# Experts' up products in halves of 32 tokens and four column groups, the second half under a branch

## What is computed

```
def _moe(h, w_router, b_router, w1, w3, w2):
    ...
    best = jnp.argmax(grp_score, axis=-1)
    in_group = (jnp.arange(N_EXPERTS) // EXPERTS_PER_GROUP)[None, :] == best[:, None]
    _, idx = lax.top_k(jnp.where(in_group, sel, -jnp.inf), TOP_K)
    ...
    for e in range(N_EXPERTS):
        he = jax.nn.silu(h @ w1[e]) * (h @ w3[e])
        out = out + gates[:, e:e + 1] * (he @ w2[e])
```

## Time and profile before

| | us |
|---|---|
| median of 3 runs (1002.15 to 1007.1) | 1004.73 |
| span of the profiled execution | 1002.4 |
| PE busy | 942.2 |
| DVE busy | 373.4 |
| ACT busy | 308.4 |
| matmuls at L900 (up), busy | 113.0 |
| matmuls at L913 (down), busy | 65.0 |

### The profile page before, as it was taken

One profiled execution on the slowest core, in us unless ns is written; L12 is line 12 of the kernel. 1 busy time (PEld: TensorE's weight loads), 2 busy tenths in 40 slices (PEclk: granted clock), 3 DMA queues, 4 the chain that ended last, 5 costly groups with the idle time before them and its releaser, 6 DMA issues.

```text
span 1002.4 us, 11949 instructions
## 1 busy us (share of the span) xinstructions
PE 942.2 (94%) x4380; PEld 513.4 (51%) x4381; DVE 373.4 (37%) x838; ACT 308.4 (31%) x700; POOL 31.7 (3%) x54
## 2 busy tenths in 40 slices
PE   3899989999999899997999999999989999999998
PEld 1455446546454335442355446455766456577763
DVE  1200497634271110522122321610855633236452
ACT  3211533332131121342233321311466632125420
POOL 0100200000000000000000002000000000000000
PEclk9999999999999999999999999999989999999999
DMA  9966482489696699899799999414226734423501
GB/s 349 364 212 229 50 314 99 157 297 336 215 365 229 216 334 393 297 396 396 276 398 383 398 396 295 178 48 157 85 84 239 215 93 168 161 91 101 133 19 42
DMA packets 105693, 230.75 MB, mean 230 GB/s; under 512 B 3124, under 2 KB 6504, under 8 KB 105496
## 3 DMA queue, kind: packets, MB, share of 16 engines
q1 hardware_dynamic: 100288, 217.85, 61.5%
q0 software_dynamic: 2208, 7.37, 2.6%
q10 hardware_dynamic: 3128, 4.62, 1.4%
HBM read 224.31 MB, written 5.51 MB: 229 GB/s over the span
## 4 chain that ended last, share of the span: by engine, by line
PE 84%; DVE 5%; ACT 4%; DMA 4%; issue 2%; SPq 1%; ACTq 0%; DVEq 0%
PE bank L633 24%; PE bank L900 12%; PE bank L647 9%; PE bank L913 6%; PE bank L930 4%; PE bank L599 3%; PE bank L1208 3%; DMA arena<-in_w_mod_dram 3%; PE bank L1137 3%; PE bank L1227 2%; PE bank L1218 2%; PE bank L829 1%; PE bank L925 1%; PE bank L762 1%; PE bank L983 1%
## 5 line engine op out<-in xcount | busy, mean ns | idle before, releaser
L633 PE MATMUL bank<-arena 128*128 128x512 f32 (+3 forms) x592 | 236.6, 558 | 1.9 <-DVE arena L2687 1.0
L633 PEld LDWEIGHTS bank<-arena 128*128 128x128 f32 x592 | 111.2, 190 | 117.9 <-issue 109.1
L900 PE MATMUL bank<-arena 128*64 128x512 f32 x512 | 113.0, 593 | 3.4 <-issue 3.4
L647 PE MATMUL bank<-arena 128*128 128x256 f32 (+1 forms) x384 | 99.3, 417 | 2.8 <-ACT arena L1935 1.5
L647 PEld LDWEIGHTS bank<-arena 128*128 128x128 f32 x384 | 72.1, 190 | 30.9 <-issue 21.7
L900 PEld LDWEIGHTS bank<-arena 128*64 128x64 f32 x512 | 38.8, 137 | 73.9 <-issue 73.3
L913 PE MATMUL bank<-arena,con 128*64 128x512 f32 x272 | 65.0, 621 | 4.6 <-ACT con L1838 4.0
L599 PE MATMUL bank<-arena,silu_c 128*32 128x512 f32 x384 | 48.8, 630 | 9.5 <-DMA arena<-in_w_mod_dram 6.7
L1739 ACT ACTIVATE con<-bank 128x256 f32<-128x256 f32 x17 | 6.5, 383 | 137.3 <-PE bank L900 137.3
L2358 DVE TENSOR_TENSOR con<-con,bank 128x256 f32<-128x256 f32 x17 | 7.2, 421 | 109.5 <-ACT con L1743 109.5
L913 PEld LDWEIGHTS bank<-arena,con 128*64 128x64 f32 x272 | 21.4, 143 | 37.6 <-issue 36.5
(11 more groups left out here) (409 smaller groups left out, 1209.8 us busy)
## 6 DMA issues: line engine op xcount, KB each, us to landing
arena<-in_w_gate_e_dram SPq DMA_DIRECT2D x16, 2048.0 KB, 14.0
arena<-in_w_up_e_dram SPq DMA_DIRECT2D x16, 2048.0 KB, 13.6
arena<-in_w_down_e_dram SPq DMA_DIRECT2D x16, 2048.0 KB, 12.4
arena<-in_w_mod_dram SPq DMA_DIRECT2D x12, 2048.0 KB, 12.0
arena<-in_mod_w_dram SPq DMA_DIRECT2D x12, 2048.0 KB, 8.0
arena<-in_ab_w_in_dram SPq DMA_DIRECT2D x7, 2048.0 KB, 9.6
arena<-in_gla_w_in_dram SPq DMA_DIRECT2D x6, 2048.0 KB, 11.1
arena<-in_cd_w_in_dram SPq DMA_DIRECT2D x6, 2048.0 KB, 7.9
```

What stands on the lines that cost most here:

```text
L633: mm = pe.matmul(ps[:, 0:n], lhs[:, k, tile * P:(tile + 1) * P], w[:, k, c0:c0 + n], start=(k == 0), stop=(k == kd_ - 1))
L647: mm = pe.matmul(ps[:, i * n:(i + 1) * n], w[:, k, c * P:(c + 1) * P], rhs[:, k, 0:n], start=(k == 0), stop=(k == KC - 1))
L900: mm = pe.matmul(up_b[64 * j:64 * j + 64, :], h[:, k, :], blocks[:, g + n:u + n + 1:u - g, :], start=(k == 0), stop=(k == KC - 1), tile_po ...
```

## The change

`up` stays for the further pass alone. An expert's own up products are made by `up_half`: 32 tokens are stationary, four column groups of 32 columns take a quarter of the hidden columns each, and 256 columns (128 of gate, 128 of up) move. The second half (tokens 32 to 63) comes first and only where a new flag, `wide_flag`, says that the expert has more than 32 tokens; this flag is now what PE reads and branches on for experts 1 to 15. Expert 0 always does both halves. The hidden values now lie in PSUM by halves, and ACT, DVE and `down` read them by other patterns with the same number of elements. In the loop of `extras` three semaphore additions stand where three drains were, and a drain stands behind the further pass. DVE makes the new flag in one operation on 128x16. ACT, DVE and POOL branch on the flags for over 64, as before.

```
+            def up_half(h, half, e, gathered=False):
+                g, u = (slot_at(s) // P for s in expert_slot[e][0:2])
+                for k in range(KC):
+                    if gathered:
+                        pe.wait_ge((hg_a, hg_v)[k % 2], k // 2 + 1)
+                    for j in range(4):
+                        n = 4 * k + j
+                        mm = pe.matmul(up_b[32 * j:32 * j + 32, 256 * half:256 * half + 256],
+                                       h[:, k, HALF * half:HALF * half + HALF], quarters[:, g + n:u + n + 1:u - g, :],
+                                       start=(k == 0), stop=(k == KC - 1), tile_position=(0, 32 * j))
+                return mm
...
-                        down(e, x_down)
+                        down(e, x_down, False)
+                        pe.drain()
                     with pe.Else():
-                        pe.drain().then_inc(x_up, 1)
-                        pe.drain().then_inc(x_turned, 1)
-                        pe.drain().then_inc(x_down, 1)
+                        pe.sem_inc(x_up, 1)
+                        pe.sem_inc(x_turned, 1)
+                        pe.sem_inc(x_down, 1)
...
-                with pe.If(any_extra > 0):
+                over_half = pe.value_load(wide_flag[0:1, e:e + 1], min_val=0, max_val=1)
+                with pe.If(over_half > 0):
                     extras(e)
+                    pe.wait_ge(hs_ready, e)
+                    up_half(hs[e % 2], 1, e)
                 with pe.Else():
                     no_extras()
                 pe.wait_ge(hs_ready, e)
-                up(hs[e % 2], e, up_done)
+                up_half(hs[e % 2], 0, e).then_inc(up_done, 1)
                 behind_up(e)
...
-                act.activation(ffT, t_b[:, 0:256].rearrange("p (c s) -> p c s", c=2), ACT.Copy).then_inc(ffT_ready, 1)
+                act.activation(ff_halves, t_b[:, 0:256].rearrange("p (a q s) -> p a q s", a=2, q=4), ACT.Copy)\
+                   .then_inc(ffT_ready, 1)
...
+            dve.tensor_scalar(wide_flag[:, :], cnt, float(HALF), None, ALU.is_gt)
```

More of the change, by code:

```diff
@@ L34 @@
 CAP = 64
+HALF = CAP // 2
 EXTRA = T // CAP - 1
@@ L218, in build @@
         extra_flag = sb("extra_flag", [P, NE, EXTRA], I32)
+        wide_flag = small[:, 352:352 + NE].bitcast(I32)
         first_slot = small[:, 288:288 + NE * (1 + EXTRA)].rearrange("p (e t) -> p e t", t=1 + EXTRA).bitcast(I32)
@@ L225, in build @@
         blocks = arena[:, :].rearrange("p (n c) -> p n c", c=256)
+        quarters = arena[:, :].rearrange("p (n c) -> p n c", c=P)
         def view(off, *dims):
@@ L274, in build @@
         act1, act2, ffT = spent[:, 0:256], spent[:, 256:512], spent[:, 512:768].rearrange("p (c s) -> p c s", c=2)
+        ff_halves = spent[:, 512:768].rearrange("p (q a s) -> p a q s", q=4, a=2)
         y_buf = [gate_rows[:, 0, 0:512], gate_rows[:, 0, 512:1024]]
@@ L891, in landed_expert, with up @@
                 pe.wait_ge(landed[expert_slot[e][j]], 16 * expert_fill[e, j])
-            def up(h, e, sem_, gathered=False):
+            def up(h, e, sem_):
                 g, u = (slot_at(s) // 256 for s in expert_slot[e][0:2])
                 for k in range(KC):
-                    if gathered:
-                        pe.wait_ge((hg_a, hg_v)[k % 2], k // 2 + 1)
                     for j in range(2):
@@ L907, in turn_ff, with down @@
                 mm.then_inc(sem_, 1)
-            def down(e, sem_):
+            def down(e, sem_, whole):
                 w2 = view(slot_at(expert_slot[e][2]), 4, D)
                 for kc in range(4):
+                    c, at = (kc // 2, 64 * (kc % 2)) if whole else (kc % 2, 64 * (kc // 2))
                     for q in range(2):
-                        mm = pe.matmul(dn_b[64 * q:64 * q + 64, :], ffT[:, kc % 2, 64 * (kc // 2):64 * (kc // 2) + 64],
+                        mm = pe.matmul(dn_b[64 * q:64 * q + 64, :], ffT[:, c, at:at + 64],
                                        w2[:, kc, 512 * q:512 * q + 512], start=(kc == 0), stop=(kc == 3),
@@ L1079, in behind_up @@
                 pe.wait_ge(ffT_ready, e + 1)
-                down(e, down_done)
+                down(e, down_done, True)
             for e in range(NE):
@@ L1085, in _ @@
                 if e == 0:
-                    up(hg[:, :, 0:CAP], e, up_done, True)
-                any_extra = pe.value_load(flags[:, e * EXTRA:e * EXTRA + 1], min_val=0, max_val=1)
-                if e == 0:
+                    up_half(hg, 1, e, True)
+                    up_half(hg, 0, e).then_inc(up_done, 1)
+                    any_extra = pe.value_load(flags[:, 0:1], min_val=0, max_val=1)
                     with pe.If(any_extra > 0):
@@ L1736, in ctx_turned, with sigmoid @@
                        .then_inc(cpT_copied, 1)
-            def sigmoid(step, at):
-                act.activation(act1, up_b[:, 0:256], ACT.Exp, scale=-1.0).then_inc(step, 1)
+            def sigmoid(step, at, gate_cols, dst):
+                act.activation(dst, gate_cols, ACT.Exp, scale=-1.0).then_inc(step, 1)
                 act.wait_ge(step, at + 1)
@@ L1805, in extras @@
                             act.wait_ge(x_up, n + 2)
-                            sigmoid(x_sig_step, n * 2).then_inc(x_silu, 1)
+                            sigmoid(x_sig_step, n * 2, up_b[:, 0:256], act1).then_inc(x_silu, 1)
                             act.wait_ge(x_turned, n + 1)
@@ L1833, in _ @@
                 act.wait_ge(up_done, e + 1)
-                sigmoid(sig_step, 2 * e).then_inc(silu_done, 1)
+                sigmoid(sig_step, 2 * e, up_b[:, :].rearrange("p (a g c) -> p g a c", a=2, g=2)[:, 0],
+                        act1.rearrange("p (a c) -> p a c", a=2)).then_inc(silu_done, 1)
                 slot0 = slot_of(act, e * (1 + EXTRA))
@@ L2355, in _, with gated @@
             flags = extra_flag[0:1, :, :].rearrange("p e t -> p (e t)")
-            def gated(sem_, value, step, at):
+            def gated(sem_, value, step, at, gate_cols, up_cols, sigmoid, dst):
                 dve.wait_ge(sem_, value)
-                dve.tensor_tensor(act1, act1, up_b[:, 0:256], ALU.mult).then_inc(step, 1)
+                dve.tensor_tensor(sigmoid, sigmoid, gate_cols, ALU.mult).then_inc(step, 1)
                 dve.wait_ge(step, at + 1)
-                return dve.tensor_tensor(act2, act1, up_b[:, 256:512], ALU.mult)
+                return dve.tensor_tensor(dst, sigmoid, up_cols, ALU.mult)
             def latent_norms(order):
@@ L2494, in extras @@
                             dve.wait_ge(x_up, n + 2)
-                            gated(x_silu, n + 1, x_gated, n).then_inc(x_ff, 1)
+                            gated(x_silu, n + 1, x_gated, n, up_b[:, 0:256], up_b[:, 256:512], act1, act2)\
+                                .then_inc(x_ff, 1)
                             dve.wait_ge(x_down, n + 1)
@@ L2514, in _ @@
                 dve.wait_ge(up_done, e + 1)
-                gated(silu_done, e + 1, up_gated, e).then_inc(ff_ready, 1)
+                both = up_b[:, :].rearrange("p (a g c) -> p g a c", a=2, g=2)
+                gated(silu_done, e + 1, up_gated, e, both[:, 0], both[:, 1], act1.rearrange("p (a c) -> p a c", a=2),
+                      act2.rearrange("p (a c) -> p a c", a=2)).then_inc(ff_ready, 1)
                 behind_ff(e)
```

## The result

The changed kernel takes 1034.84 us (median of 5 runs, 1028.9 to 1042.74) against 1004.73 before (1001.3 to 1007.1): the ratio is 1.0298, 95% interval 1.0264 to 1.0332. I had forecast 1019.6 and a range up to 1030: slower, as said, but by twice as much, and outside the range. The profiled execution is the slowest of the five, 7.9 us above the median, so what is read from it is somewhat larger than what the median holds.

A forecast was written before the change was run, and what follows sets the result against it. PE was taken to bound the experts' stage, with full DMA queues as close. Savings in narrow experts, less empty loops, clock and weight waits, put the last `down` 14.9 us later: 1004.7 + 14.9 = 1019.6, range 1004 to 1030.

The forecast's parts named there:

- The half: Own up products on PE: one half of 64 passes takes 3.45 us, both 6.9 as before; nine narrow experts save 3.45 each.
- The turn: Empty loop in experts 5, 6, 7, 10, 11: 1.85 us a turn, 6.8 from weights to first product.
- The clock: PE's granted clock falls after gaps at the loops: 1.5 us charged to the up behind each, bounds 0 and 3.4.
- Code loading: Jumps of the loops waiting for code packets of 1.1 us each: priced at 5.5 us more, left out of the sum.
- The walk: Start times followed from expert 5 (402.3) through expert 15: last `down` ends at 621.7 instead of 606.8, +14.9 us.
- The hidden loop: Rival: empty turns cost next to nothing on PE's path, so the kernel is faster, about -16.5 us, 988; chance 0.11.
- the cancelling: Rival: gain and loss cancel with turns of 1.5 us and no slow clock, -1.5 us, 1003; chance 0.07.
- Slow halves: Rival: four column groups miss their pace at 256 columns, +4.6 us, 1024, at the upper bound 1065; chance 0.07.
- The code rival: Rival: code loading stalls the jumps of the loops, +5.5 us, 1025 or more; chance 0.07.
- The other side of the prediction: Experts' stage: PE has 1.5 us or less to spare on weights; narrow experts 9 and 12 to 14 gain nothing.

The follow-up runs named there:

- Run 2: Changed kernel with both halves computed in every expert and the further pass under its own flag, so no empty loops; 1014.54 us, ratio 1.0101.
- Run 5: Changed kernel with the further pass's flag read inside the wide branch, so no empty loops while the long jump stays; 1016.94 us, ratio 1.0153.
- Run 8: Changed kernel with four useless products in each empty loop turn to keep PE busy; 1029.43 us, ratio 1.0264.
- Run 1: Kernel before, with one half's 16 products added inside the branch that only expert 8 takes; 1026.02 us, ratio 1.0206.
- Run 7: Changed kernel with the common half first, the second half in its own branch, and the further pass's body in experts 0 and 8 alone; 1002.38 us, ratio 0.9999.
- Run 6: Changed kernel with the further pass under its own flag, the common half first, then the second half in its own branch; 1004.33 us, ratio 1.0005.
- Run 10: Run 7's kernel with half of each expert's down weights not transferred, a sixth of the experts' bytes; 992.8 us, ratio 0.9899.

## Why the prediction was wrong

- **The half** (3.45 us, both 6.9). Right within 0.2: 3.66 with the way through the array and 3.59 to the next work; both halves 7.11 against 7.07 before. (The next work behind expert 15 starts at 599.40, not 599.3, so an up held PE for 6.97.) Run 2 shows that pace isn't the loss. What I costed at nothing, more instructions for the same work, may be the 10 us that run 2 loses; that is argued.
- **The turn** (1.85 us; 6.8 from the weights to the first product). Right: 1.9, and 6.7 in expert 5. Run 5 takes the loops out and gains 17.9.
- **The clock** (1.5 us behind each loop). Under-sized. The wide ups behind loops took 8.80 to 10.03 against 7.11, 2.3 on the mean of experts 5, 6, 7, 8, 10 and 11; `down` of expert 8 (6.38 against 3.65) and the narrow halves behind stalls had no term at all. Run 8 does not price the part behind the loops: its 5.4 us hold the stalls that went with it.
- **Code loading** is the step that failed: "in the one loop that ran, branches took at most 0.21 us and none waited, so the sum leaves it out". I took the rule of the Trainium skill ("Runtime: NRT & Kernel Launch", Instruction fetch mechanics: a taken branch to a page that isn't in the current two waits for it) for a rule on the loop's jumps back. They never stalled here. The rule bites the forward jump, which every narrow expert takes and which the change made longer, 6.08 to 6.22 us in four of them, each with a packet of code within it; on that the trace agrees with the Trainium skill. I looked for the price where the change added branches and not where it put code under one already there. The trace before had a first sign, the 1.41 us of expert 0's forward branch. Run 1 prices the longer jump in the kernel before: 22.2 us, of which 3.5 are expert 8's own half. The packet of 1.1 us that I took for the price is only the transfer; a stall took 4 to 6 us.
- **The walk.** It was off from its first step. Expert 5 started at 414.4 and not 402.3: two stalls of 3.87 ahead of experts 3 and 4, and halves that took 6.32 and 5.06 instead of 3.66, 11.8 together. Expert 1 was 3.0 late besides, and part of the loop ran behind `down`. I had let narrow experts 1 to 4 reach expert 5 on time for sure. From there to expert 7 it held its distance (11.0); expert 8's second start was at 499.6, 16.0 late, and expert 11's up ended 19.6 late, most of these further 7.5 us being the clock's. Its waits for weights were right: expert 10's passes 20.9 behind expert 8's up (taken 21.0), expert 15's 57.1 behind expert 11's (taken 54.1). The last `down` ended at 645.9 against 621.7, in the slowest of the five executions. So about half of the miss of 24.2 is the two stalls at experts 3 and 4; those at 9 and 12 to 14 stood ahead of waits for weights and cost 3 us at most.
- **Rivals.** The hidden loop and the cancelling fell (turn of 1.9, slow clock). Slow halves fell (run 2). The code rival was right in kind, though not in the jumps it named, and had 0.07 and a quarter of the price that run 1 measured.
- **The other side of the prediction held**: weights limit what faster narrow experts can give. Run 7, with no empty loop, almost no stall of a branch and nine halves saved, gets 0.0% with the full bytes and 1.3% under the kernel before with the cut ones (992.8 against 1005.87, 13 us, of which I had said 12 or more).

The parts are not additive. Taking out the loops gives 17.9, the long jumps 12.2, and runs 6 and 7, with no empty loop and no branch over 1.3 us behind expert 0's, 30.5 and 32.5: about the whole loss. None of the versions beats the kernel before with all weights transferred. That none could by much is an inference from the waits of runs 7 and 10 and not shown.

## What to carry to other kernels

Code under a branch is not free for those who skip it. Count what the skipped side crosses in instructions, and compare the jump's 4 to 6 us with the work that it saves (here 3.45). Put the common work ahead of the branch and not behind it: with the common half first the same jump did not stall (0.43 us at most). And look at the queue that fills the next stage before shortening this one: where it is full, saved time comes back as a wait that the profile calls issue.

## What I had not expected of the hardware

- A taken forward branch of 6.0 to 6.2 us on PE's sequencer, in some experts and not in others of the same code length; a few instructions moved elsewhere change which (experts 3, 4, 9, 12 in the changed kernel; 2, 3, 4, 9, 13, 14 without the empty loops; 3 alone in run 8). Of such a branch the packet of code is 1.1 us; 3.6 to 3.7 pass ahead of it and 1.4 behind it.
- A jump over only one half stalled 4.5 us when another taken jump stood 1.4 us ahead of it.
- Straight code can stall too: 2.02 us in the middle of expert 13's half, again ended behind a packet of code.
- A stall can be paid twice: behind expert 3's the granted clock was 1.2 GHz, so 3.87 idle and 2.66 more for a half of 3.66. Behind expert 9's (3.49 idle) the half took its 3.66.
